# Taking the idle products out of a two-block transformer kernel, behind its first projections

## The reference

```
x = layer_norm(ALPHA * x + (1.0 + g1) * y, ln_g[l, 0], ln_b[l, 0])
h = modulate(x, sh2, sc2)
y = sq_relu_mlp(h, mlp_w1[l], mlp_w2[l])
x = layer_norm(ALPHA * x + (1.0 + g2) * y, ln_g[l, 1], ln_b[l, 1])
...
u = rms_norm_2(h, norm_mix_pre[l]);  proj = u @ w_in[l]
mix = concatenate([o_dn, o_at]) @ w_out[l];  h = h + rms_norm_2(mix, norm_mix_post[l])
u = rms_norm_2(h, norm_mlp_pre[l])
f = square(relu(u @ w_up[l])) @ w_down[l];  h = h + rms_norm_2(f, norm_mlp_post[l])
```

## Time and profile before

| | us |
|---|---|
| median of 3 runs | 1154.88 |
| lowest and highest | 1152.62, 1156.89 |
| the profiled execution | 1154.68 |
| its span, first to last instruction | 1152.9 |
| mean granted TensorE clock | 0.980 |

### The profile page before, as it was taken

One profiled execution on the slowest core, in us unless ns is written; L12 is line 12 of the kernel. 1 busy time (PEld: TensorE's weight loads), 2 busy tenths in 40 slices (PEclk: granted clock), 3 DMA queues, 4 the chain that ended last, 5 costly groups with the idle time before them and its releaser, 6 DMA issues.

```text
span 1152.9 us, 20471 instructions
## 1 busy us (share of the span) xinstructions
PE 1095.7 (95%) x8417; PEld 974.4 (85%) x8417; DVE 761.2 (66%) x1282; ACT 608.9 (53%) x1102; POOL 65.5 (6%) x84
## 2 busy tenths in 40 slices
PE   6999989999999999889999999998789999999997
PEld 3989567999899899879999988998668888999986
DVE  1786877899987775578655447874876557444443
ACT  2544756543544556656455555466664345565453
POOL 0012770000000000000000000110000000000000
PEclk8999999999999999999999999999789999999999
DMA  9997116899997354336856551250000045555540
GB/s 371 406 395 319 38 43 250 308 362 358 343 355 264 139 209 165 113 126 213 328 188 219 183 182 40 99 231 2 1 2 21 5 180 184 194 188 183 183 147 36
DMA packets 33564, 218.30 MB, mean 189 GB/s; under 512 B 4528, under 2 KB 5296, under 8 KB 8896
## 3 DMA queue, kind: packets, MB, share of 16 engines
q1 hardware_dynamic: 33472, 217.00, 50.9%
HBM read 215.93 MB, written 1.05 MB: 188 GB/s over the span
## 4 chain that ended last, share of the span: by engine, by line
PE 76%; DVE 11%; ACT 7%; DMA 2%; POOL 2%; issue 1%; DVEq 0%; SPq 0%; ACTq 0%
PE bank L527 20%; PE bank L529 20%; PE bank L528 20%; DVE low L521 2%; ACT high L515 2%; DMA ring<-ada_halves 2%; POOL zb L1141 1%; PE bank L567 1%; PE bank L644 1%; PE bank L2455 1%; PE bank L2457 1%; DVE y_tmp L1607 1%; PE bank L582 1%; PE bank L2443 1%; DVE stats L1609 1%
## 5 line engine op out<-in xcount | busy, mean ns | idle before, releaser
L521 DVE TENSOR_TENSOR low<-ring,high 128x2048 fp32r<-128x2048 f32 (+1 forms) x139 | 317.6, 2287 | 242.2 <-ACT high L515 241.8
L515 ACT ACTIVATE high<-ring 128x2048 fp32r<-128x2048 f32 (+1 forms) x139 | 264.7, 1906 | 247.5 <-PE bank L529 199.5
L527 PE MATMUL bank<-act_high,high 128*128 128x256 f32 (+1 forms) x1072 | 308.3, 288 | 0.0
L529 PE MATMUL bank<-act_high,low 128*128 128x256 f32 (+1 forms) x1072 | 303.8, 283 | 0.0
L528 PE MATMUL bank<-act_low,high 128*128 128x256 f32 (+1 forms) x1072 | 303.6, 283 | 0.0
L527 PE MATMUL bank<-high,act_high 128*128 128x512 f32 (+1 forms) x632 | 233.7, 370 | 3.2 <-DVE act_low L3005 1.8
L529 PE MATMUL bank<-high,act_low 128*128 128x512 f32 (+1 forms) x632 | 231.2, 366 | 0.0
L528 PE MATMUL bank<-low,act_high 128*128 128x512 f32 (+1 forms) x632 | 231.2, 366 | 0.0
L527 PEld LDWEIGHTS bank<-act_high,high 128*128 128x128 f32 x1072 | 205.0, 191 | 4.5 <-issue 2.4
L528 PEld LDWEIGHTS bank<-act_low,high 128*128 128x128 f32 x1072 | 205.0, 191 | 2.4 <-issue 1.4
L529 PEld LDWEIGHTS bank<-act_high,low 128*128 128x128 f32 x1072 | 204.9, 191 | 0.0
(11 more groups left out here) (511 smaller groups left out, 1384.1 us busy)
## 6 DMA issues: line engine op xcount, KB each, us to landing
ring<-chunks SPq DMA_DIRECT2D x138, 1024.0 KB, 5.0
ring<-ada_halves SPq DMA_DIRECT2D x38, 1024.0 KB, 5.1
o_land<-ada_halves SPq DMA_DIRECT2D x6, 1024.0 KB, 11.9
ring<-raw_cmp SPq DMA_DIRECT2D x4, 1024.0 KB, 11.5
x_tok<-ada_halves SPq DMA_DIRECT2D x3, 1024.0 KB, 15.1
gate_rows<-ada_b SPq DMA_DIRECT2D x4, 512.0 KB, 9.9
bias<-bias_by_distance SPq DMA_DIRECT2D x1, 2048.0 KB, 13.2
ln_rows<-ln_g SPq DMA_DIRECT2D x4, 512.0 KB, 6.0
```

Of the source, the lines that this page charges most:

```text
L515: e.activation(weights(c)[0], in_ring(("w", c)), ACT.Copy).then_inc(*act.up("high", c))
L521: e.tensor_tensor(low, in_ring(("w", c)), high.bitcast(F32), ALU.subtract).then_inc(*vec.up("low", c))
L527: e.matmul(out_, ah, bh, start=start, stop=False)
L529: return e.matmul(out_, al, bh, start=False, stop=stop)
```

## The change

All calls of `keep_running` behind the first projections go, and with them the table `IDLE`. The calls in the norms (L1562, L1564, L2194, L2196, L2902, L2909), the one for chunk (0, 2) (L2434) and the one for `rot` (L2706) together issue 134 of the kernel's 169 idle products. The 35 of the first projections stay.

```
-        IDLE = {"y0": (0, 10, 6), "m0": (0, 10, 6), "y1": (0, 10, 6), "b2": (12, 26, 6), "y2": (0, 7, 3)}
...
             for t in range(QT):
-                keep_running(e, IDLE[tag][t], tag, t)
                 features_tensor(e, tag, t, n_tok[:, t, :], NORM_PUTS[t], made=(vec, act))
-            keep_running(e, IDLE[tag][QT], tag, QT)
...
             for t in range(QT):
-                keep_running(e, IDLE["b2"][t], "b2", t)
                 features_tensor(e, "b2", t, n_tok[:, t, :], PUTS[t])
-            keep_running(e, IDLE["b2"][QT], "b2", QT)
...
-            if k == (0, 2):
-                keep_running(e, 12, "x", k)
...
-                    if t == 1:
-                        keep_running(e, 20, "rot", t)
...
             for t in range(QT):
-                keep_running(e, IDLE["y2"][t], "y2", t)
...
-            keep_running(e, IDLE["y2"][QT], "y2", QT)
             mlp_tensor(e, "m2", MLP2, {}, "y2")
```

## The result

| us | before | after |
|---|---|---|
| median | 1154.41 (6 runs) | 1163.40 (6 runs) |
| lowest, highest | 1152.38, 1156.89 | 1161.82, 1167.75 |
| profiled execution | 1154.68 | 1161.82 |
| its span | 1152.9 | 1160.0 |
| mean granted clock | 0.980 | 0.962 |

The changed kernel is slower by a ratio of 1.0071, 95% interval 1.0053 to 1.0090, some 8 us (the medians lie 9.0 apart).

A forecast was written before the change was run, and what follows sets the result against it. TensorE's own speed was taken to bound most stages, VectorE and ScalarE the norms and delta rule. Clock losses of 6.0 + 1.0 + 2.5 + 1.5 = 11.0 us on 1154.7 gave 1165.7 us, range 1158 to 1172.

The forecast's parts named there:

- The direct gain: Whole kernel: removing the idle products saves almost nothing, since TensorE is idle behind them; only 0.3 us at y1 (0 to 0.5).
- Rival 1: At y0, m0 and y2 the clock holds at the short gaps; 4.5 us lost in all, 1159.2 us; chance 0.17.
- rival 2: Low clock lies within the norms, where TensorE waits anyway, so not slower: -0.9 us, 1153.8 us; chance 0.06.
- The price of a norm like y0: At y0, m0 and y2: each loses 2.0 us to a clock fall, bounds 0 and 3.9.
- The prediction had named this other course: At a norm: the low stretch may begin inside it, costing less, but a second may follow, as from 802.0 to 808.9.
- y1 at 1.0 us: At y1: 2.0 us, less 0.7 already lost there and 0.3 direct gain; bounds -0.5 and 3.0.
- b2 at 2.5 us: At b2: low clock costs 0.5 us for transposes on the chain and 2.0 for products; bounds 0 and 4.0.
- The delta rule at 1.5 us: Delta rule: products on the chain between the existing low stretches run at half speed, about 1.5 us more; bounds 0 and 5.
- The upper bound: Delta rule: 5 us; of 117 records 67 are idle, and the other 50 would take 5.5 us more if all on the chain.
- The sum, 11.0 us: Whole kernel: 6.0 + 1.0 + 2.5 + 1.5 us lost, giving 1165.7 us; term bounds add to -0.5 and +23.7.
- Rival 3: Everywhere the clock comes back late, two low stretches after each norm: 21.7 us lost, 1176.4 us; chance 0.11.
- What the mean clock says: Whole span: mean clock 0.98 taken to agree with the Trainium skill's ramp penalty under 1%, a loss under 11.5 us.

## Why the prediction was right

- **The direct gain is next to nothing: right.** At `m0`, where the clock held until 393.2, the way from the first transposes (387.97 before, 387.98 after) to L543 (394.90, 394.91) is the same to 0.01 us without the products. The gaps behind the first transposes are the predicted ones: 3.09 us for 3.1 at `y0`, 4.00 for 4.0 at `y1`, 6.51 for 6.5 at `b2`, 7.20 for 7 in the delta rule, 2.23 for 2.3 at `y2`.
- **The loss lies at the start of each stage: right.** From the first product of the MLP to the last, the three MLPs took 1.3, 1.6 and 2.1 us longer, all of it while the clock was low; behind that the shift stays the same to 0.02 us. No time is lost in the middle of an MLP.
- **The clock falls at all norms: right**, in both traces, and in that of one product each. Rival 1, that it holds at the short gaps, is refuted by the kernel with only those norms changed; rival 2 by the ratios of the changed kernel and of the one with one product each. The one doubtful place, `y2`, fell too.
- **The price of a norm like y0, 2.0 us: right.** `y0`, `m0` and `y2` took 1.8, 2.0 and 2.1 us in the profiled execution, and 2.2, 2.7 and 0.9 in the second. The working behind it counted one stretch of 3.4 us, all in dense products, and 0.4 us for transposes. What came were mostly stretches of 6.8 us that began inside the norm, so that about half of each lay in waiting, and the transposes were slow at `y0` but not at `m0` and `y2`. The prediction had named this other course, but that both come to 2.0 us is in part luck.
- **y1 at 1.0 us: low.** It took 1.75 and 1.26. The stretch was 10.2 us long; I had set off one stretch of 3.4 us against it. The 0.3 us of direct gain can't be told from the slow transposes there.
- **b2 at 2.5 us: right in size**, 2.2 in both traces (in the second without the fall at 753), and 2.8 in that of this one alone.
- **The delta rule at 1.5 us: mis-sized.** The transposes of `rot` and the products behind them do take 1.4 us more, as worked out, but 0.7 to 0.8 us come back behind it, mostly at the end of the low stretch that before has from 860.1 to 866.9. Alone it is 0.7 us in the trace and nothing in the runs. The upper bound rests on a miscount: from 808.9 to 826.0 the idle records are 64 (40 and 24), not 67, and 53 are left, not 50. The clock was also not low without a break from 802 to 840: it was at 1.00 from 813.1 to 816.5 and from 826.7 to 830.1.
- **The sum, 11.0 us: near, and on the high side.** The places took 10.5 us in one pair of traces. The profiled executions differ by 7.1 because before's trace has a fall at 491 that after's lacks, and a start that is 1.8 us longer, with a fall at 20. The runs give 8.2 us by the ratio, and 9.8 and 9.7 in the later runs of this kernel and of the one with one product each. The term that the runs don't show is that of the delta rule, 1.5. Rival 3 had each norm at its upper bound; none but `y1` in length came near it, and its sum of 21.7 was not seen.
- **What the mean clock says: misread.** The prediction took 0.98 as agreeing with a loss of under 1%. It can't show that: it is 2% of the clock, 23 us of 1152.9 if all of it lay in dense work, and what part of it did was not measured.

Not foreseen was how much the clock does where nothing was edited: falls at 99, 172, 491, 741 to 756 and 880 to 886 are in some traces and not in others. By the shifts they are worth 0.9, 1.2, 1.6, 1.0 to 2.6 and 1.5 us. That is as much as one norm. Two traces of the same kernel differ in such falls (491 and 753, in the changed one); but in the kernels with only some norms changed the extra loss is in all executions, so not all of it is chance. The shares of the places hold for the traces that they are read from, and can't be taken for what each place would lose alone.

## What to carry to other kernels

Idle products pay where TensorE waits for other engines between two stages in which it is the bound. Read off the gap behind the last real product and fill it. Here a gap was worth some 2 us (0.9 to 2.9 by the traces) with all or most of the gaps open; kernels with only some of them open lost more than their share, so measure the set and not the piece. Where another engine bounds what follows, as in the delta rule here, the products are worth nothing that can be measured. Check what else the run takes: one idle product that took a PSUM bank at the wrong place cost 3.6 us. And compare kernels between marks, stretch by stretch, with the clock's falls beside them, before two spans are compared.

## What the runs showed of the hardware

- The granted clock falls at places where it did not in another execution of the same instructions (at 494 and 753 in the second trace of the changed kernel, not in the first), and a low stretch lasts from 3.4 to 27.3 us. While it is low, the MLP's products of 256 columns take 0.42 us in place of 0.28. Half as many idle products keep the clock at some gaps and not at others (`m0` held, `y0` did not).
- Float32 transposes of the identity keep the clock up less than as many products of the same shape and length: in two traces they held it at `m0` both times, at `y0` once and at `b2` and `y2` never, where the products held it at all four, and the time was 1.0037 to 1.0052 of before.
- At the start TensorE runs at its slower pace, and idle products end that sooner: eight records of products of 512 columns take 1.94 us at 6.28 and 1.06 at 13.15 in the trace of before; without any idle products eight take 1.93 us at 13.30 and the 32 records at 33.51 take 8.34 us, for 5.58 before, and the first change of the clock stands at 39, while the profile writes 1.00 for want of a record.
